# Pool projections and first gate moved into the recurrence's block, outer product on VectorE, modulation batches in the middle of each gate's product

## The reference, cut to what matters

```
mod = c @ ada_w + ada_b                      # six groups of 1024: sh1, sc1, g1, sh2, sc2, g2
h = layer_norm(x) * (1 + sc1) + sh1
proj = h @ w_in                              # r, k, v, three loras | pool (512) | gate_pool | gate_rwkv
y_rwkv = rwkv7(r, w, k, v, kk, a)            # recurrence in t per head; then group norm, bonus, gate
S = S * w - sa (kk * a) + v k^T              # the 8 samples: one step each, with an outer product v k^T
pooled = mean over windows 2/4/8/16 of p_in, minus p_in, @ pool_w * pool_scale
merged = sigmoid(gate_pool) * (pooled @ w_branch_pool) + sigmoid(gate_rwkv) * (y_rwkv @ w_branch_rwkv)
mix = merged @ w_out
x = layer_norm(ALPHA * x + (1 + g1) * mix);  then the convolutional FFN with sh2, sc2, g2
```

## Time and profile before

| | us |
|---|---|
| median of three runs | 1270.6 |
| profiled execution | 1269.56 |
| its span, first to last instruction | 1267.8 |
| PE busy (matmul) | 1137.2 |
| VectorE busy | 705.6 |
| ScalarE busy | 486.8 |
| GpSimd busy | 107.3 |

### The profile page before, as it was taken

One profiled execution on the slowest core, in us unless ns is written; L12 is line 12 of the kernel. 1 busy time (PEld: TensorE's weight loads), 2 busy tenths in 40 slices (PEclk: granted clock), 3 DMA queues, 4 the chain that ended last, 5 costly groups with the idle time before them and its releaser, 6 DMA issues.

```text
span 1267.8 us, 34796 instructions
## 1 busy us (share of the span) xinstructions
PE 1137.2 (90%) x15404; PEld 1034.9 (82%) x15404; DVE 705.6 (56%) x1126; ACT 486.8 (38%) x800; POOL 107.3 (8%) x153
## 2 busy tenths in 40 slices
PE   3967999999999997589999999789998999779995
PEld 1356888888888885489999999689998999779995
DVE  2134665666666755378712554866757665633226
ACT  0335533534445333333343323555343534422221
POOL 0000220211302202020000000500000000000000
PEclk9969999999999999699999999899999999989998
DMA  8330220220220100456895733133222222342321
GB/s 258 139 101 8 54 58 5 57 58 3 58 57 4 41 3 5 149 135 179 221 261 162 214 104 97 50 96 89 83 83 83 83 87 79 102 136 80 90 68 68
DMA packets 185119, 117.49 MB, mean 93 GB/s; under 512 B 6324, under 2 KB 177130, under 8 KB 184705
## 3 DMA queue, kind: packets, MB, share of 16 engines
q1 hardware_dynamic: 184993, 115.57, 31.1%
HBM read 108.40 MB, written 7.34 MB: 91 GB/s over the span
## 4 chain that ended last, share of the span: by engine, by line
PE 31%; DVE 9%; issue 8%; ACT 6%; DMA 2%; DVEq 1%; ACTq 0%; POOL 0%; SPq 0%; POOLq 0%
PE PJ L231 24%; PE PJ L223 4%; ACT Wh L1625 2%; ACT ACC L1823 2%; DVE ACC L2219 2%; DVE ACC L2220 1%; DVE ACC L2227 1%; PE BB L1397 1%; DVE ACC L2225 1%; DMA RAW<-in_w_in_dram 1%; ACT ACC L1821 1%; DVE Wl L1873 1%; DMA RAW<-in_w_branch_rwkv_dram 1%; ACT SFh L1830 1%; DVE DF L1906 1%
## 5 line engine op out<-in xcount | busy, mean ns | idle before, releaser
L231 PE MATMUL PJ<-Hh,Wh 128*128 128x260 f32 (+2 forms) x1184 | 263.6, 304 | 34.5 <-DVE Wl L1873 16.9
L231 PE MATMUL PJ<-Hh,Wl 128*128 128x260 f32 (+2 forms) x1184 | 242.5, 287 | 1.4 <-issue 1.4
L231 PE MATMUL PJ<-Hl,Wh 128*128 128x260 f32 (+2 forms) x1184 | 242.9, 287 | 0.0
L231 PEld LDWEIGHTS PJ<-Hh,Wh 128*128 128x128 f32 x1184 | 186.6, 192 | 55.8 <-issue 28.1
L1873 DVE TENSOR_TENSOR Wl<-RAW,Wh 128x1024 fp32r<-128x1024 f32 (+2 forms) x108 | 125.6, 1165 | 161.9 <-ACT Wh L1625 157.1
L231 PEld LDWEIGHTS PJ<-Hh,Wl 128*128 128x128 f32 x1184 | 187.1, 192 | 1.6 <-issue 1.6
L231 PEld LDWEIGHTS PJ<-Hl,Wh 128*128 128x128 f32 x1184 | 186.6, 192 | 0.0
L1625 ACT ACTIVATE Wh<-RAW 128x1024 fp32r<-128x1024 f32 (+2 forms) x112 | 113.2, 1014 | 148.6 <-PE PJ L231 99.9
L2219 DVE SCALAR_TENSOR_TENSOR ACC<-ACC,CP 128x512 f32<-128x512 f32 x88 | 66.1, 751 | 71.5 <-ACT ACC L1823 69.9
L1172 POOL TENSOR_TENSOR MO<-BP,CST 128x512 f32<-128x512 f32 x40 | 55.7, 1400 | 307.2 <-DVE KP L1055 250.4
L231 PE MATMUL PJ<-SFh,Wh 128*128 128x256 f32 (+1 forms) x308 | 64.4, 291 | 13.5 <-DVE Wl L1873 13.5
(11 more groups left out here) (365 smaller groups left out, 2146.8 us busy)
## 6 DMA issues: line engine op xcount, KB each, us to landing
RAW<-in_w_in_dram SPq DMA_DIRECT2D x46, 512.0 KB, 5.2
RAW<-in_ffn_up_dram SPq DMA_DIRECT2D x44, 512.0 KB, 3.8
AD<-in_ada_w_dram SPq DMA_DIRECT2D x21, 512.0 KB, 5.6
RAW<-in_ffn_down_dram SPq DMA_DIRECT2D x16, 512.0 KB, 4.0
RAW<-in_ada_w_dram SPq DMA_DIRECT2D x11, 512.0 KB, 5.7
RAW<-in_ada_w_dram SPq DMA_DIRECT2D x2, 2048.0 KB, 10.7
ACC<-in_ada_w_dram SPq DMA_DIRECT2D x2, 2048.0 KB, 13.6
RAW<-in_w_branch_rwkv_dram SPq DMA_DIRECT2D x8, 512.0 KB, 4.9
```

Source lines behind the costliest of these rows:

```text
L231: mm = pe.matmul(out[:, b, 0:nb[b]], w[:, slot, kw, :], x[:, kx, c0:c0 + nb[b]], start=first and w is Wh and x is xh, stop=last and w is Wl)
```

## The change

It makes the last slot like the others and moves work into its waits:

- `dense` runs in slot 7 too: 24 k-steps of pool projections 0 to 2 (numbers 26 to 28). Pool projection 3 and gate 0 are run after it, around `center` and `variance`, which now write to banks B[0] and B[1]. ScalarE's `pooled(q)` copies the projections to PN, four tiles laid over SW, WL, A2 and what follows, and the splits and `lo`s of numbers 26 to 31 move along. SP loads numbers 26 to 33 in this block.
- The next block starts with gate 1 and has mix 0 behind gate 1, mixes 1 and 2 behind gate 2, mix 3 in the middle of gate 3.
- `ada_batch(p)` stands between the fourth and fifth k-step of gate p, from p = 3 (before: behind the product, from p = 1), so the last batches are those behind the pooled-branch products e = 0 to 3 (before 0 and 1). The YGh/YGl work moves to e = 4 to 7.
- SP's iteration p loads `B_GATE + 4 + p`, with the same two modulation loads behind it.
- VectorE forms the outer product itself, half by half into TA; GpSimd's instruction is gone. The first two `lo_n` of the sample recurrence move ahead of it.
- The samples' state (2 MB) is written out after the loop, no longer in iteration 10.

```diff
 # PE, recurrence's block
                     def dense(n):
-                        if not nxt:
-                            return
...
                 center(KT - 1, False)
+                project(B_POOL + 3, 1, 0, 2)
                 variance(KT - 1)
+                project(B_POOL + 3, 1, 2, KT)
+                project(B_GATE, 0, 0, KT)
 # SP, recurrence's block
-                    if c < KT - 1:
-                        block_in(c + 1, K_)
+                    block_in(c + 1, K_)
+                block_in(KT, R_)
+                block_in(KT, V_)
                 wkv_out(KT - 2)
+                for n in range(B_POOL + 3, B_POOL + 6):
+                    w_load(sp, n, slot_of(n), cols("in", 26 + n - B_POOL), ring=2 if n < B_POOL + 5 else 5)
+                w_load(sp, B_GATE + 2, slot_of(B_GATE + 2), cols("in", 32))
                 wkv_out(KT - 1)
+                w_load(sp, B_GATE + 3, slot_of(B_GATE + 3), cols("in", 33))
 # ACT, end of the recurrence's block
                 center(KT - 1)
+                split(B_GATE)
+                pooled(2)
                 roots(KT + 2, slice(TN, TN + T), ("lnv", KT))
+                pooled(3)
+                split(B_GATE + 1)
 # SP, next block
-                for n in range(B_POOL, B_POOL + 3):
-                    load(n)
                 sp.dma_start(PW[:], ...)
                 sp.dma_start(S0[:]..., i["state_wkv"]...)
-                load(B_POOL + 3)
+                load(B_GATE + 4)
                 sp.wait_ge(S("vt"), 1)
                 (VEC x6, RKB x3)
-                for n in range(B_GATE, B_GATE + 4):
-                    load(n)
                 for n in range(3):
                     load_ada(n)
                 for p in range(1, NG):
-                    load(B_GATE + 3 + p)
+                    load(B_GATE + 4 + p)
                     for n in (2 * p + 1, 2 * p + 2):
                         if n < NA:
                             load_ada(n)
-                    if p == 10:
-                        sp.wait_ge(S("s_new"), 1)
-                        sp.dma_start(o["wkv_s"]..., S0...)
...
+                sp.dma_start(o["wkv_s"]..., S0...)
-                for n in range(B_GATE + 3 + NG, B_OUT):
+                for n in range(B_GATE + 4 + NG, B_OUT):
                     load(n)
 # PE, next block
                 def ada_batch(p):
-                    if p >= 2:
+                    if p == 4:
+                        pe.wait_ge(S("mf"), NPOOL)
+                    if p >= 4:
                         for n in range(2):
-                            ada_turn(2 * (p - 2) + n)
-                    if p <= NA // 2:
+                            ada_turn(2 * (p - 4) + n)
+                    if p <= NA // 2 + 2:
                         for n in range(2):
-                            ada_rows(2 * (p - 1) + n)
+                            ada_rows(2 * (p - 3) + n)
-                for p in range(NG):
+                for p in range(1, NG):
                     for k in range(KT):
+                        if k == KT // 2 and p >= 3:
+                            if p == 3:
+                                mix(pe, 3)
+                            ada_batch(p)
                         mm = kstep(...)
 # ACT, next block: for gate p
                     act.activation(two(gate), PJ[p % 2][:, :, 0:260], ACT.Sigmoid)
                     split_n(B_GATE + 3 + p)
-                    if p == 0:
-                        mixed(NPOOL - 1)
+                    if p == 1:
                         (PO copy)
+                        mixed(0)
+                    elif p == 2:
+                        mixed(1)
+                        mixed(2)
-                    else:
+                    elif p > 2:
+                        if p == 3:
+                            mixed(3)
                         ada_batch(p)
 # ACT, pooled branch
                     split_n(B_PB + 3 + e)
-                    if e < 2:
+                    if e < 4:
                         ada_batch(NG + e)
-                        if e < 6:
-                            for c in range(2 * (e - 2), 2 * (e - 2) + 2):
-                                act.activation(YGh[:, c, :], YG[:, c, :], ACT.Copy)
+                        for c in range(2 * (e - 4), 2 * (e - 4) + 2):
+                            act.activation(YGh[:, c, :], YG[:, c, :], ACT.Copy)
 # DVE, next block
+                pooled(0)
+                lo_n(B_GATE + 2)
+                pooled(1)
+                pooled(2)
+                lo_n(B_GATE + 3)
+                mix_lo(0)
+                mix_lo(1)
+                pooled(3)
+                mix_lo(2)
+                lo_n(B_GATE + 4)
+                mix_lo(3)
-                lo_n(B_GATE + 3)
                 read(SA, 0, VKK)
-                lo_n(B_GATE + 4)
                 decay(0)
                 lo_n(B_GATE + 5)
                 renew(0)
 # in renew
-                    step(dve.tensor_tensor(vals(S0, h), vals(S0, h), vals(TB, h), ALU.add))
+                    step(dve.tensor_tensor(TA[:], VEC[:, VV, ...]..., row(VK), ALU.mult))
+                    stepped_all()
+                    step(dve.tensor_tensor(vals(S0, h), vals(S0, h), TA[:], ALU.add))
 # POOL
-                pool.tensor_tensor(TB[:], VEC[:, VV, :]..., VEC[:, VK, :]..., ALU.mult)
```

More of the change, by code:

```diff
@@ L481, in build @@
             WK = sb("WK", [P, C], ctx=sc)
+            PN = [place(n, [P, PB + TN], over) for n, over in (("PN0", "SW"), ("PN1", "WL"), ("PN3", "A2"))]
+            PN.insert(2, place("PN2", [P, PB + TN], "A2", PB + TN + 1))
             I2 = CST[:, C_I2:C_I2 + C]
@@ L832, in shift, with pooled @@
                     act.activation(A2[:, T:TN], PJ[pj][:, 1, 260:268], ACT.Copy, scale=m).then_inc(S("sh"), 1)
+                def pooled(q):
+                    act.wait_ge(S("prj"), B_POOL + q + 1)
+                    act.activation(two(PN[q][:, PB:PB + TN]), PJ[q % 2][:, :, 0:260], ACT.Copy).then_inc(S("pn"), 1)
                 def split(n):
-                    slot = n % 3
-                    act.wait_ge(S(f"w_load{slot}"), 16 * (n // 3 + 1))
-                    after(act, "prj", n - 2)
+                    slot = slot_of(n)
+                    act.wait_ge(S(f"w_load{slot}"), loads_of(n))
+                    after(act, "prj", n - 2 if n < B_POOL + 3 else min(n - 1, B_POOL + 3))
                     act.activation(Wh[:, slot], RAW[:, slot], ACT.Copy).then_inc(S("w_hi"), 1)
@@ L933, in slot @@
                         gates(c + 1)
+                    else:
+                        split(B_POOL + 3)
                     act.wait_ge(S("mm_y"), c + 1)
@@ L1075, in slot @@
                             shift(num(c + 1, K_), 0, XK, om(c + 1, K_))
[L1076 removed]
+                        if lv == 4 and nxt:
                             lo(num(c + 2, K_))
@@ L1106, in slot @@
                                                      ALU.mult, ALU.add).then_inc(S("s"), 1)
+                        if j == 1 and not nxt:
+                            lo(B_POOL + 3)
                         if j == 0 and nxt:
@@ L1146, in _ @@
                 group_floor(KT - 1)
+                lo(B_GATE)
                 for step in range(3):
                     group(KT - 1, step)
+                lo(B_GATE + 1)
             @block.gpsimd
@@ L1369, in mix @@
                 pe.wait_ge(S("df"), g + 1)
-                after(pe, "mf", g)
+                after(pe, "mf", g if g != 2 else 0)
                 for b in range(2):
-                    mm = pe.matmul(B[2 + b][:, 0:260], PW[:, g, :], DF[:, 260 * b:260 * b + 260], start=True, stop=True)
+                    mm = pe.matmul(B[MIX_B[g] + b][:, 0:260], PW[:, g, :], DF[g % 2][:, 260 * b:260 * b + 260], start=True, stop=True)
                 mm.then_inc(S("mm_mix"), 1)
@@ L1380, in _ @@
                 mm.then_inc(S("t_vt"), 1)
-                for q in range(NPOOL):
-                    n = B_POOL + q
-                    pe.wait_ge(S("w_lo"), n + 1)
-                    after(pe, "pn", q - 1)
-                    for k in range(KT):
-                        mm = kstep(pe, PJ[q % 2], slot_of(n), k, Hh, Hl, k, k == 0, k == KT - 1)
-                    mm.then_inc(S("prj"), 1)
-                    if q > 0:
-                        mix(pe, q - 1)
                 def ada_rows(n):
@@ L1644, in _ @@
                 v.then_inc(S("vt"), 1)
-                for q in range(NPOOL):
-                    act.wait_ge(S("prj"), B_POOL + q + 1)
-                    act.activation(PN[:, q, PB:PB + TC].rearrange("p (a b) -> p a b", a=2), PJ[q % 2][:, :, 0:HC], ACT.Copy).then_inc(S("pn"), 1)
-                    split_n(B_POOL + 3 + q)
-                    if q > 0:
-                        mixed(q - 1)
+                split_n(B_GATE + 2)
                 def ada_mod(n):
```

171 lines of the change are left out of this document (83 added, 88 removed).

## The result

The kernel after took 1325.4 us, median of four runs (1323.4 to 1330.6), beside 1270.55 us for the kernel before: ratio 1.044, 95% interval 1.041 to 1.048. It is 54.8 us slower by the medians, 56 by the ratio. Its profiled execution spans 1322.7 us, before 1267.8.

The account below looks back on a forecast made before the run. PE, busy 90% of the span, bounds the kernel, so its standstills and low clock count. -31.9 + 6.3 + 44.7 + 21.7 + 8.0 = +48.8 on 1269.6 gives 1318.4 us; range 1284 to 1338.

Parts of the forecast that it names:

- Gate 1: Later block's first gate: after slot 7 (47.4), tail (14.0) and change of block (1.2) it starts at 537.5, -31.9 us.
- Start of the gates: Gate 1's start to batch 3's end: number 35 lands near G+17, mix 3 runs at G+24.7; +6.3 us.
- Batch 3 to batch 15: Gates' stage: VectorE's late lo of number 35, then periods of 11.0 us; 133.2 instead of 88.5, +44.7 us.
- the circle: Gates: batch q waits for the load batch q-1 released, through ScalarE's split and copies; period 10.7 to 11.6, before 7.3.
- rival 1: Gates: the circle doesn't bind, gates run at 7.3 us; 1258, or 1266 with the late lo of number 35; chance 0.05.
- Pooled branch: Batches 16 to 18 are in the circle too, 18 behind the written 2 MB; 47.6 instead of 25.9, +21.7 us.
- Rwkv branch: Last YGh/YGl pair queues behind number 56's split and lo, so PE stops in the first product; +8 us.
- Later work: Everything after the rwkv branch's third product: a chain on PE that shifts as it stands.
- Rival 2: Gates: weights land sooner, with the modulation tiles, 5.3 us after issue; period about 8.1, time 1287; chance 0.08.
- Rival 3: Gates: each wait leaves a whole period at 1.2 GHz, period 14.6; +32 us more, 1356 with the branch; chance 0.07.

Follow-up runs that it names:

- experiment 5: Kernel after, with the last YGh/YGl pair ahead of number 56's split and lo: 1322.7 us, ratio 1.039.
- experiment 1: Kernel after, with SP issuing each weight load one iteration earlier, ahead of the modulation loads that wait for batch p+2: 1276.25 us, ratio 1.004.
- experiment 2: Kernel after, with ScalarE copying the modulation rows before it splits the coming weights, SP's order as changed: 1276.55 us, ratio 1.003.
- experiment 6: Kernel after, with weight loads one iteration earlier and the last YGh/YGl pair ahead of number 56's split and lo: 1269.1 us, ratio 1.000.
- experiment 10: Kernel after with loads earlier, YG pair first, state written early, gates' start reordered, batches behind products, lo of number 36 ahead of renew(0): 1249.05 us, ratio 0.985.

## Why the prediction was right

Forecast 1318.4, measured 1325.4, by the mechanism it named. Step by step:

- **Gate 1** began at 539.2, forecast 537.5. The tail took its 14.0, slot 7 48.4 instead of 47.4, and the slots before it ended 1.0 later. The gain is 30.2 instead of 31.9.
- **Start of the gates**: +9.7 (31.3 less 21.6) instead of +6.3. The order was right, the landing of number 35 was 2.7 us later than priced. I had priced it by the bytes ahead of it at 0.3 MB/us. It was also late by its issue. A load n waits only for VectorE's `lo` of number n - 3 (not for a split, as I wrote of `w_load`), and that was done by 542.7, but SP was still issuing what stands before it. These rows show SP's queue and then the split on ScalarE:

```profile
540.49 6.98 SPq L1326 DMA_DIRECT2D VEC<-VT  x6
...
551.81 1.72 SPq L218 DMA_DIRECT2D RAW<-in_w_in_dram  x1
```

```profile
558.94 1.06 ACT L1647 ACTIVATE Wh<-RAW 128x1024 fp32r<-128x1024 f32 x1 [6.18 <-DMA RAW<-in_w_in_dram]
```

The next two rows are the stretch in which SP issued the VEC transfers and the 4.3 us behind it (the last three numbers are clock, DMA share and GB/s):

```profile
540.50:547.50 7.00, 7.00 (x58) 6.78 (x57) 5.93 (x13) 4.35 (x5) 0.00 (x0) 1.00 0.96 357
547.50:551.80 4.30, 4.30 (x38) 4.30 (x37) 2.60 (x7) 2.89 (x5) 0.00 (x0) 1.00 0.50 123
```

So beside the VEC issues bytes did bind, and only the 4.3 us behind them left the engines half idle, about 2 us of transfer by estimate. From 538.3 to 559.0 they were 0.86 busy at 258 GB/s. The load was issued 12.6 us after the gates began and was there at 19.7, not 17; mix 3 ran at 27.4, not 24.7.
- **Batch 3 to batch 15**: 133.2, as forecast. The period from batch 6 to 13 is (683.43 - 606.44) / 7 = 11.0, the two after it 8.9 and 9.7. That the stage matches to 0.1 us is luck: I had chosen 11.0 out of 10.7 to 11.6, single turns scatter by 1 us, and experiment 5's took 6.4 us more from batch 6 to 18 with the same circle. Its parts were 1.25, 7.73 and 1.59 in the turn shown, for 0.9 to 1.8, 8.1 and 1.7. (The "1.2 us at most" that ScalarE waited before the change holds for the eight turns of the earlier trace rows; in the ninth, the one of 8.9 us, it waited 1.90.) Experiments 1 and 2 show by two separate cuts that it is the circle. They took away 50.8 and 51.8 us by the ratios (0.0400 and 0.0408 of 1270.6); forecast and rival 1 lie 1318 - 1266 = 52 apart, and both measured ends are 7 to 10 us above theirs.
- **Pooled branch**: +25.5 instead of +21.7. The turns of batches 16 and 17 took 9.7 and 9.1 (forecast 9.8 each), that of 18 13.8 instead of 12.3. The rest took 18.8 from 736.3, with PE busy throughout at a clock of 0.85; at full clock that is 16.0. This low clock after a wait of 7.6 was missing in the sum, 2.8 us, and is the largest part of what this branch missed.
- **Rwkv branch**: +7.8 instead of +8. The wait of 9.76 came from the queued YGl pair, as named; experiments 5 and 6 moved it away and brought back the 2.5 us for the third product.
- **Later work** shifted as it stood, but 2.6 us shorter (1322.7 - 777.5 = 545.2, before 547.8). Sum: -30.2 + 9.7 + 44.7 + 25.5 + 7.8 - 2.6 = +54.9, the difference of the spans. The forecast of this difference was +48.8; the misses are +1.7, +3.4, 0, +3.8, -0.2 and -2.6, and the last, which nothing here explains, made the total look better.

**The rivals.** Rival 1, that the circle doesn't bind, is what experiments 1 and 2 built; it gave 1276, not 1258 to 1266. In experiment 1's trace the start cost +9.6 instead of +6.3 and the pooled branch +13.0 (38.9 us) instead of +6, with the written state and low clock in it. Rival 2, that weights land with the tiles in front of them, would give a period of 8.1. Rival 3, a whole period at low clock, would need 14.6; it was 11.0. The Trainium skill (TensorE: Matmul & The Clock Gate, HAM oscillation) describes a loop whose turns each begin at low clock after a wait for a DMA. The trace agrees in part. Here are the turns of batches 7 to 10, with the clock as third number from the end:

```profile
617.20:627.80 10.60, 9.13 (x85) 8.70 (x85) 6.71 (x5) 2.33 (x7) 0.00 (x0) 0.84 0.56 148
627.80:639.40 11.60, 9.07 (x85) 8.50 (x85) 6.19 (x6) 2.31 (x7) 0.00 (x0) 0.85 0.49 137
639.40:651.00 11.60, 10.61 (x85) 9.90 (x85) 1.79 (x5) 2.30 (x7) 0.00 (x0) 0.71 0.49 138
651.00:661.60 10.60, 7.57 (x85) 7.15 (x85) 1.25 (x2) 2.34 (x7) 0.00 (x0) 1.00 0.55 148
```

Three are in part at low clock, one isn't. The turns at 0.84 and 1.00 are equally long, for the slower matmuls fill what would be waiting. That is also why PE's waits, at 0.6 to 3.2 us, were smaller than the 2.5 to 3.5 that I named: the period is set by the circle, and PE splits it between low clock and idle time. Low clock costs in the part of PE's work that lies on the circle: in the turn at 0.71 this took 2.10 us instead of 1.25, and that turn was 11.6 us long. (So was the turn at 0.85, by a landing of 8.8 us instead of 7.7.) ScalarE stood 1.6 to 3.8 us before each split, where I had named about 4.

**What the parts are worth**, by differences of ratios and medians, each good to 4 or 5 us by the intervals: the circle 51, the queued YG pair 5 to 7, the state's late write 9 to 11 by the timed runs (5.6 in the traces), the order at the start 4 (runs of 1260.0 to 1261.3 and 1251.6 to 1258.5). Without these four, the same change, with its batches behind the products, took 1250 us, 1.7% (1.3 to 2.0) faster than the kernel before: the gate that starts 30 us earlier is real. From gate 1 to the rwkv branch experiment 10 takes 10.8 us longer than the kernel before (146.8, before 705.4 - 569.4 = 136.0). Of them 4.8 are the mixes and PN transposes that were ahead of gate 1 before (four of 1.04 and one group of 0.60), 5.2 are four waits left on PE (2.67, 0.41, 1.48, 0.67), the first behind the sample recurrence's half-state steps. Finer pieces of those steps between the `lo`s weren't tried.

## What to carry to other kernels

When a step of one engine is moved by one or two turns of a loop, count for every load which turn releases it and which turn consumes it, through all in-order queues it stands in, SP's included; where the distance falls from two turns to one and the sum of the latencies is longer than the engine's own work in a turn, that sum becomes the period, however much bandwidth is left (here 10.6 to 11.6 us for 7.3, with the DMA engines 0.51 busy). Before moving a wait, write down what is queued behind it on the same engine: here the 50 us came from two ordinary lines (a load behind a released load, a copy behind a split), and changing either of them was enough. And price a small edit in a kernel that isn't bound by a latency circle, or the circle's scatter covers it.

## What the runs showed of the hardware

- One VectorE instruction with two inputs was held through all of a GpSimd instruction with two inputs: 7.03 us for 8 elements beside GpSimd's 7.06, 0.17 without it. The Trainium skill (GPSIMD Engine Reference, 1. Specifications) has the two share an interface, with contention when VectorE's instruction has two SBUF inputs; the trace agrees.
- Issuing six small transfers (VEC from VT, 32 KB each) held SP's queue for 6.98 us in the kernel after and 4.36 in the kernel before, 0.60 to 1.85 us each, where many a load of 512 KB took 0.37. The DMA engines were 0.96 to 0.99 busy in both stretches, so what makes these issues long isn't shown.
- A group of two modulation tiles and a weight tile, 1.5 MB, took 7.7 us from the first issue to the weights' use in one turn and 9.7 in another kernel's turn of the same form; the periods of the circle scatter from 10.6 to 11.6 in one kernel and up to 13.1 in another.
- The clock that PE gets inside such a circle changed from turn to turn (0.71 to 1.00). Turns at 0.84 and at 1.00 were equally long, 10.6 us; of the 1 us by which the turn at 0.71 was longer, 0.85 was PE's own part of the circle at 1.2 GHz.
